# Key/value, query and recurrent output products taken from high and low parts of their operands

## What is computed

```
h = x
layer 0: xn = rms_norm(h);  q, f, i, g = split(xn @ hgrn_w_in)        # 1024 x 4096
         o  = chunkwise gated recurrence(silu(q), key(f), i, decay(f))  # 8 heads of 128
         h += (rms_norm(o) * silu(g)) @ hgrn_w_out                      # 1024 x 1024
         h += swiglu(rms_norm(h))                                       # dense, 2816 wide
shared:  kv = rms_norm(h) @ kv_w                                        # 1024 x 1536
         compressed, selected and window keys and values from kv
layer 1: proj = rms_norm(h) @ nsa_w_in                                  # 1024 x (1024 + 48 gates)
         h += attention(three branches, gated) @ nsa_w_out
         h += top-2-of-8 experts (each 3584 wide) of rms_norm(h)
```

## Time and profile before

| | us |
|---|---|
| median of 3 runs (1558.01 to 1558.24) | 1558.22 |
| the profiled execution's own time | 1556.34 |
| its span, first to last instruction | 1554.8 |
| TensorE (PE) busy | 1521.5 (98%) |
| VectorE (DVE) busy | 1127.9 (73%) |
| ScalarE (ACT) busy | 938.3 (60%) |
| GpSimd (POOL) busy | 56.2 (4%) |
| mean granted clock of TensorE | 0.996 |

### The profile page before, as it was taken

One profiled execution on the slowest core, in us unless ns is written; L12 is line 12 of the kernel. 1 busy time (PEld: TensorE's weight loads), 2 busy tenths in 40 slices (PEclk: granted clock), 3 DMA queues, 4 the chain that ended last, 5 costly groups with the idle time before them and its releaser, 6 DMA issues.

```text
span 1554.8 us, 19505 instructions
## 1 busy us (share of the span) xinstructions
PE 1521.5 (98%) x6905; PEld 1182.5 (76%) x6905; DVE 1127.9 (73%) x988; ACT 938.3 (60%) x946; POOL 56.2 (4%) x83
## 2 busy tenths in 40 slices
PE   7999999999999998999999999999999999999998
PEld 6866578887455647888888888888888888888886
DVE  1077455554326837888888889888888888888997
ACT  4323344443213435778778778778778778778775
POOL 2000100000101001000000000000000000000100
PEclk9999999999999999999999999999999999999999
DMA  9833155448575017999999999999999999999994
GB/s 363 282 109 100 53 179 202 170 148 218 200 296 189 1 35 262 378 369 367 396 388 357 395 384 356 394 382 365 393 388 357 393 386 355 394 394 348 398 393 181
DMA packets 213023, 455.53 MB, mean 293 GB/s; under 512 B 9857, under 2 KB 36522, under 8 KB 212970
## 3 DMA queue, kind: packets, MB, share of 16 engines
q1 hardware_dynamic: 206624, 441.48, 78.2%
q0 software_dynamic: 3536, 12.96, 2.1%
q10 hardware_dynamic: 2810, 0.40, 0.1%
HBM read 434.89 MB, written 19.92 MB: 293 GB/s over the span
## 4 chain that ended last, share of the span: by engine, by line
PE 95%; DVE 3%; POOL 1%; issue 0%; DMA 0%; ACT 0%; DVEq 0%; POOLq 0%
PE bank L2079 59%; PE bank L1714 8%; PE bank L1731 4%; PE bank L1608 4%; PE bank L1641 4%; PE bank L1777 3%; PE bank L1946 2%; PE bank L1630 2%; PE bank L1664 2%; PE bank L2099 2%; PE bank L1840 1%; PE bank L1814 1%; DVE small L1308 1%; PE bank L1915 1%; PE bank L1888 1%; POOL small L539 0%
## 5 line engine op out<-in xcount | busy, mean ns | idle before, releaser
L1467 DVE TENSOR_TENSOR w_lo<-ring,w_hi 128x2048 fp32r<-128x2048 f32 x333 | 756.3, 2290 | 104.8 <-ACT w_hi L900 104.1
L900 ACT ACTIVATE w_hi<-ring 128x2048 fp32r<-128x2048 f32 x333 | 638.0, 1921 | 169.6 <-PE bank L2079 166.5
L2079 PE MATMUL bank<-w_hi,x_hi 128*128 128x512 f32 x896 | 244.3, 394 | 0.6 <-DVE x_lo L1475 0.6
L2079 PE MATMUL bank<-w_hi,x_lo 128*128 128x512 f32 x896 | 240.0, 390 | 0.0
L2079 PE MATMUL bank<-w_lo,x_hi 128*128 128x512 f32 x896 | 239.7, 389 | 0.0
L2079 PEld LDWEIGHTS bank<-w_hi,x_lo 128*128 128x128 f32 x896 | 168.2, 188 | 35.9
L2079 PEld LDWEIGHTS bank<-w_lo,x_hi 128*128 128x128 f32 x896 | 168.2, 188 | 35.2
L2079 PEld LDWEIGHTS bank<-w_hi,x_hi 128*128 128x128 f32 x896 | 164.5, 188 | 32.3 <-issue 0.8
L1073 DVE TENSOR_TENSOR ring_lo<-ring,f_whi 128x1024 fp32r<-128x1024 f32 x66 | 80.6, 1225 | 87.0 <-ACT f_whi L734 87.0
L2079 PE MATMUL bank<-w_hi,t_hi 128*128 128x512 f32 x448 | 122.6, 395 | 0.0
L2079 PE MATMUL bank<-w_hi,t_lo 128*128 128x512 f32 x448 | 121.1, 392 | 0.0
(11 more groups left out here) (276 smaller groups left out, 1486.3 us busy)
## 6 DMA issues: line engine op xcount, KB each, us to landing
ring<-in_moe_w_gu SPq DMA_DIRECT2D x224, 1024.0 KB, 7.6
ring<-in_moe_w_down SPq DMA_DIRECT2D x112, 1024.0 KB, 8.1
ring<-in_ffn_w_gu SPq DMA_DIRECT2D x22, 1024.0 KB, 6.5
ring<-in_hgrn_w_in SPq DMA_DIRECT2D x16, 1024.0 KB, 15.3
ring<-in_ffn_w_down SPq DMA_DIRECT2D x10, 1024.0 KB, 6.9
x_rows<-arena SPq DMA_DIRECT2D x2, 4096.0 KB, 21.6
ring<-in_kv_w SPq DMA_DIRECT2D x6, 1024.0 KB, 6.2
ring<-in_hgrn_w_out SPq DMA_DIRECT2D x4, 1024.0 KB, 11.1
```

Source lines behind the costliest of these rows:

```text
L900: act.activation(w_hi[s % PARTS][:, :], raw[:, s % RAWS, :], ACT.Copy).then_inc(hi_ready, 1)
L1467: dve.tensor_tensor(w_lo[s % PARTS][:, :], raw[:, s % RAWS, :], w_hi[s % PARTS][:, :].bitcast(F32), ALU.subtract).then_inc(lo_ready, 1)
L2079: last = mm(out_, x_[k], w[:, k, 512 * b:512 * b + 512], start=start and k == 0 and n == 0, stop=stop and k == HALF // width - 1 and n == 2)
```

## The change

The three plain products are taken from parts as well: each 8 matmuls of a product become 24, in two halves of 12 (four `k`, three kinds). Weights are parted in quarters of an item (128x1024).

- Recurrent output: ACT makes eight high quarters behind its copies of rounds 4 to 7 of the recurrence, into slots 4 and 5; DVE subtracts them in rounds 5 to 8, one behind each group's `ops_ready`. The low part of the rows is made by DVE, one step of 128x512 for each quarter of the rows, behind `on_ready`. Items 11 and 12 of the dense weights, which go into these slots, wait for the third and the fourth output product.
- Keys and values: ACT makes the rows' high part (`rows_high`) once all of the dense layer's output is there, DVE the low part, and the high weight quarters lie in the arena (the first six) and in slots whose item has been used (free at `kv_ps` 2 and 4, ...). The last four transposes of h stand inside the first product. `cin` waits for `kv_ps` 4 as well.
- Queries: high and low parts of the rows are copies of 128x1024 each, twice, behind `kv_ps` 6; the eight weight quarters follow `kv_ps` 4 to 6.
- POOL clears its block only behind `kv_ps` 4; SP issues the zeroing ahead of the output weights; these now wait for `q_ps` 4, and so do the first expert weights (before: `q_ps` 3).
- The small transfers are issued later, in round 2 of ACT's key/value loop; positions stay on `misc_in` (32), the other three go to `wr_in`, awaited just ahead of the gates.

```diff
         def left(i):
+            if i in (4, 5):
+                return res_ps, i - 1
...
             if i < I_CMP:
-                return kv_ps, 2 * (i - I_KV) + 2
+                return q_ps, 4
...
+            pool.wait_ge(kv_ps, 4)
             pool.memset(b_zero, 0.0).then_inc(zero_made, 1)
...
+                if n >= 4:
+                    for s in (2 * n - 8, 2 * n - 7):
+                        if s < 8:
+                            i = I_HOUT + s // 4
+                            act.wait_ge(slot_full[i % SLOTS], full(i))
+                            act.wait_ge(proj_ready, 10 + 2 * (s // 4))
+                            act.activation(o_quarter(s)[2], o_quarter(s)[0], ACT.Copy).then_inc(o_hi, 1)
...
+            def weight_high(*ss):
+                for s in ss:
+                    i = n_item(s)
+                    act.wait_ge(slot_full[i % SLOTS], full(i))
+                    act.wait_ge(*n_free(s))
+                    act.activation(n_high(s), n_quarter(s)[0], ACT.Copy).then_inc(q_hi, 1)
...
+            weight_high(0, 1, 2, 3)
+            rows_high(0)
+            rows_high(1)
+            rows_high(2)
+            rows_high(3)
             squared(2, 0, 6)
             squared(2, 1, 8)
+            weight_high(4, 5)
+            act.wait_ge(xT_dve, 8)
             shared_turned(1, G_MIX1, xT)
+            act.wait_ge(xT_dve, 10)
             shared_turned(3, G_MIX1, xT)
             for j in range(6):
+                if j == 1:
+                    weight_high(6, 7)
+                if j == 2:
...
+                    weight_high(8, 9)
...
+                if j == 3:
+                    weight_high(10, 11)
+                if j == 4:
+                    weight_high(12, 13)
                 act.wait_ge(kv_ps, j + 1)
...
+            query_rows_high(0)
+            weight_high(14, 15)
+            query_rows_high(1)
+            weight_high(16, 17, 18, 19)
...
+                    if 5 <= n:
+                        s = 2 * (n - 5) + grp
+                        dve.wait_ge(o_hi, s + 1)
+                        dve.tensor_tensor(o_quarter(s)[1], o_quarter(s)[0], o_quarter(s)[2].bitcast(F32),
+                                          ALU.subtract).then_inc(o_lo, 1)
...
+            weight_low(0, 1, 2)
             residual(4, 0)
             residual(4, 1)
-            shared_turned(0, G_KV, b_xk)
             residual(4, 2)
             residual(4, 3)
-            shared_turned(2, G_KV, b_xk)
+            weight_low(3)
+            rows_low(0)
+            rows_low(1)
+            rows_low(2)
+            rows_low(3)
             shared_turned(0, G_MIX1, xT)
+            weight_low(4, 5)
             shared_turned(2, G_MIX1, xT)
+            weight_low(6, 7)
...
+            dve.wait_ge(kv_ps, 2)
+            weight_low(8, 9)
             key_normed(0)
+            weight_low(10, 11)
...
+            weight_low(12, 13)
             key_turned(0)
             key_normed(2)
             key_turned(1)
+            query_rows_low(0)
+            weight_low(14, 15)
             key_normed(3)
+            query_rows_low(1)
+            weight_low(16, 17)
             key_turned(2)
             key_turned(3)
+            weight_low(18, 19)
...
             def shared(j):
                 it, tb = divmod(j, 2)
+                for a in range(2):
+                    s = 4 * it + 2 * a
+                    if j == 0 and a == 1:
+                        turned(2)
+                        turned(3)
+                    pe.wait_ge(q_hi, N_QUART + s + 2)
+                    pe.wait_ge(f_x_ok, 4 + 2 * tb + a + 1)
+                    wh, wl = halves_of_item(s)
+                    for kind, (x_, w) in enumerate(((n_xhi, wh), (n_xhi, wl), (n_xlo, wh))):
+                        if kind == 1:
+                            pe.wait_ge(q_lo, N_QUART + s + 2)
+                        if kind == 2:
+                            pe.wait_ge(xT_dve, 6 + 2 * tb + a + 1)
+                        for k in range(4 * a, 4 * a + 4):
+                            last = mm(bank[:, KV_BANK[j], :], x_[:, k, P * tb:P * tb + P], w[k % 4], ...)
```

More of the change, by code:

```diff
@@ L771, in shared_turned, with rows_high @@
                 last.then_inc(xT_act, 1)
-            shared_turned(1, G_KV, b_xk)
-            shared_turned(3, G_KV, b_xk)
+            def weight_high(*ss):
[4 more added lines that the diff above has]
+                    act.activation(n_high(s), n_quarter(s)[0], ACT.Copy).then_inc(q_hi, 1)
+            def rows_high(j):
+                tb, k0 = j // 2, 4 * (j % 2)
+                act.wait_ge(res_ps, 8)
+                act.wait_ge(xT_ps, 9 + j)
+                for k in range(k0, k0 + 4):
+                    last = act.activation(n_xhi[:, k, P * tb:P * tb + P], bank[:, j, P * (k - k0):P * (k - k0) + P],
+                                          ACT.Copy, scale=gain[:, G_KV + k:G_KV + k + 1])
+                last.then_inc(f_x_ok, 1)
@@ L775, in _, with query_rows_high @@
+            def query_rows_high(half):
+                act.wait_ge(kv_ps, 6)
+                act.wait_ge(xT_dve, 12)
+                act.wait_ge(xT_act, 4)
+                act.activation(q_xhi[:, 4 * half:4 * half + 4, :], xT[:, 4 * half:4 * half + 4, :],
+                               ACT.Copy).then_inc(f_x_ok, 1)
+            weight_high(0, 1, 2, 3)
[3 more added lines that the diff above has]
+            rows_high(3)
             squared(2, 0, 6)
             squared(2, 1, 8)
+            weight_high(4, 5)
@@ L1066, in _ @@
                                   ALU.mult).then_inc(on_ready, 1)
+                for i in {1: (0,), 2: (1,), 3: (2, 3)}.get(j, ()):
+                    dve.wait_ge(oT_act, i + 1)
+                    at = slice(4 * (i % 2), 4 * (i % 2) + 4), slice(P * (i // 2), P * (i // 2) + P)
+                    dve.scalar_tensor_tensor(o_xlo[:, at[0], at[1]], bank[:, 4 + i, :].rearrange("p (k t) -> p k t", k=4),
+                                             gain[:, G_HG:G_HG + 1], o_xhi[:, at[0], at[1]].bitcast(F32),
+                                             ALU.mult, ALU.subtract).then_inc(oT_lo, 1)
             quarters = [0]
@@ L1211, in _ @@
             dve.wait_ge(pos_ready, 1)
+            dve.wait_ge(kv_ps, 4)
             for g in range(NG):
@@ L1766, in _, with turned, halves_of_item @@
                 down_quarter(f)
-            for j in range(4):
+            def turned(j):
                 pe.wait_ge(h_ready, 5 + j)
                 turn_block(h, j // 2, 4 * (j % 2), j, xT_ps)
+            turned(0)
+            turned(1)
+            def halves_of_item(s):
+                high, low = [], []
+                for d in (s, s + 1):
+                    for v, to in ((n_high(d), high), (n_quarter(d)[1], low)):
+                        to += [v[:, 512 * k:512 * k + 512] for k in range(2)]
+                return high, low
             def shared(j):
                 it, tb = divmod(j, 2)
-                if tb == 0:
-                    arrived(I_KV + it)
-                for k in range(KD):
-                    last = mm(bank[:, KV_BANK[j], :], b_xk[:, k, P * tb:P * tb + P], cols(I_KV + it)[:, k, :],
-                              start=k == 0, stop=k == KD - 1)
+                for a in range(2):
+                    s = 4 * it + 2 * a
[6 more added lines that the diff above has]
+                    for kind, (x_, w) in enumerate(((n_xhi, wh), (n_xhi, wl), (n_xlo, wh))):
+                        if kind == 1:
+                            pe.wait_ge(q_lo, N_QUART + s + 2)
+                        if kind == 2:
+                            pe.wait_ge(xT_dve, 6 + 2 * tb + a + 1)
+                        for k in range(4 * a, 4 * a + 4):
+                            last = mm(bank[:, KV_BANK[j], :], x_[:, k, P * tb:P * tb + P], w[k % 4],
+                                      start=k == 0 and kind == 0, stop=k == KD - 1 and kind == 2)
                 last.then_inc(kv_ps, 1)
@@ L1978, in _ @@
             turn(0)
-            query(3, range(4, 8))
+            query(3, (1,))
             copied(0)
```

141 lines of the change are left out of this document (101 added, 40 removed).

## The result

| | before | after |
|---|---|---|
| median (lowest to highest of 4 runs each), us | 1558.12 (1557.66 to 1558.24) | 1546.68 (1545.51 to 1547.52) |
| ratio of the two, 95% interval | | 0.9932 (0.9919 to 0.9945) |
| the profiled execution's own time, us | 1556.34 | 1545.51 |
| its span, us | 1554.8 | 1543.9 |
| mean granted clock of TensorE in it | 0.996 | 0.994 |

The forecast was 1545.7 us; the change is faster by 11.4 us (1558.12 - 1546.68), where 12.5 were forecast. That it lies so near is partly luck, and it hides two errors: the keys, values and queries gave what they should, the recurrence gave less (1.4 us instead of 2.3), and a stretch that was to stay as it is, the attention, grew by 1.4 us.

The account below looks back on a forecast made before the run. TensorE, busy 98% of the span, was taken as the bound. Savings of 2.3 (recurrence), 6.9 (keys, values) and 3.3 (queries) sum to 12.5: 1558.22 - 12.5 = 1545.7 us, range 1543.5 to 1548 (8 in 10: 1541 to 1551.5).

Parts of the forecast that it names:

- Price of a product: Each changed product: 24 matmuls at 0.231 us take 5.55 us instead of 6.87, saving 1.32.
- Recurrent output: Recurrence to dense start: four products save 5.3 us, last round loses 2.6, before the last half 0.4; net 2.3 saved.
- the walk: Recurrence's last round, step by step: ACT's exponentials 0.6 us late, last pairs at 157.6, first output product 2.6 late.
- The rival of the falling clock: Clock falls where TensorE idles in the recurrence's last round: up to 2 us lost, 1547.5 us; chance 0.20.
- its 0.4: Recurrent output, before the last half: DVE makes two low row quarters before the addition the next transposes need; 0.4 us lost.
- Keys and values: Six products save 1.32 us each, 0.8 gained at the start, 0.7 and 1.1 lost to waits; net 6.9 saved.
- the third item's low quarters: Keys and values: DVE makes them behind the first key's norm, which waits for POOL; TensorE loses 1.1 us.
- that of the second item: Keys and values: TensorE waits for the second item's late quarters because ACT runs late; 0.7 us lost.
- Queries: First two products save 1.32 us each, the third's second half 0.66, the fourth nothing; sum 3.3 saved.
- From here everything moves together: After the queries, the attention onward merely starts earlier; the DVE chain there is untouched, no change in length.
- Hidden parts: Zeroing, output and expert weights, and small transfers stay hidden at zero cost; compression's blocks ready by less than 1 us.
- four signs of being wrong: Matmuls above 0.24 us, clock below 1 around 157, weight waits in the SwiGLU's second chunk, or a longer attention.

Follow-up runs that it names:

- warm_tail: Changed kernel plus ten zero-weight matmuls between the two groups of pairs of the recurrence's last round; median 1544.90 us, 0.9928 of before.
- again: The changed kernel itself, unedited, measured once more on another chip; median 1547.90 us, 0.9939 of before.
- pool_early: Changed kernel with POOL clearing its block behind the second product of keys and values instead of the fourth; median 1547.92 us, 0.9937 of before.
- warm_attn: Changed kernel plus ten zero-weight matmuls at the attention's start, where TensorE idles behind the last query product; median 1542.82 us, 0.9916 of before.
- q3_one: Changed kernel with the fourth query product from high parts alone, 8 matmuls instead of 24; median 1546.28 us, 0.9931 of before.
- all_three: Changed kernel with the edits of tail_moved, pool_early and warm_attn together; median 1540.75 us, 0.9890 of before; repeated on a third chip, 1540.97 us, 0.9904.
- tail_moved: Changed kernel with the last two high quarters and DVE's two subtractions moved out of the recurrence's last round; median 1544.41 us, 0.9918 of before.
- all_filled: all_three with gate matmuls split around half the first query product, warm_tail's filling, and eight zero matmuls at the attention's second idle place; 1540.80 us, 0.9898 of before.

## Why the prediction was right, and where not

**Price of a product: right.** 5.51 to 5.55 us for 24 matmuls. The trace has 0.230 us a matmul. An estimate by the 215.7 ns of the Trainium skill (TensorE: Matmul & The Clock Gate, Part 1, "Wait — 56ns, not 53.3ns?") would have had 5.18 (24 x 0.2157), 6% too low for this type.

**Recurrent output: the mis-sized term.** Forecast -2.3 us, measured -1.4. Each step of the walk came out (0.41 for 0.6, pairs at 157.54 for 157.6), and the working priced the matmuls behind them at the full clock. The rival of the falling clock had 0.20 and 0.9 to 2 us; here the two groups took 0.92 (2.08 - 1.16) and 0.66 (1.57 - 0.91) longer, partly beside other work, and warm_tail wins back 0.66 of the stage. With the clock up, that is, the part gives 2.07 (47.56 - 45.49). The other 0.2 of the miss is not the clock's: one half of a product runs while ACT and DVE work toward the next transposes (from 188.41 to 192.42 before, from 187.77 to 191.78 after, 4.01 us both times), so that making it cheaper gains nothing, and seven halves give 4.6 us (7 x 0.66) where 5.3 - 0.4 = 4.9 was in the sum. The forecast's reason for its 0.4, DVE's low quarters of the rows ahead of the addition, does not show. All five profiled executions whose last round is as changed and unfilled have this fall (after, again, pool_early, warm_attn, q3_one), and of the other seven changed versions only one (all_three). The forecast had the idle stretch (152.5 to 159.5) and the row that shows what follows one, and still left it out of the sum. It should have been in the sum, and the last two quarters out of the last round: tail_moved shows that the choice of place, with the fall that it brings, not the product from parts, cost 3.2 us of 4.6 that the four products could give (47.56 - 42.92).

**Keys and values: right.** Forecast -6.9, measured -7.05. The first product starts 1.82 us behind the SwiGLU's end (386.11 - 384.29), forecast 1.7. The wait for the third item's low quarters is 1.03 us against 1.1; that of the second item, forecast at 0.7, does not show among TensorE's waits. It was overstated by ACT's walk, which is a little faster than the 1.1 us a quarter I took (1.99 for two in the chain).

**Queries: right.** Forecast -3.3, measured -3.45; q3_one confirms that the fourth product is worth nothing.

**"From here everything moves together": failed.** The attention is 76.46 us before and 77.84 after. Of its instructions only those of the last query product changed, with which TensorE is done sooner: it idles 2.48 us behind it, where in the kernel before its idle time was 1.14. Four marks in it show what the clock takes: the first scores, the matmul behind this idle time, the one behind the second (2.00 us in both kernels), and the end. Without a fall (warm_tail) the parts are 16.94, 9.41 and 48.31 us. Before has 16.92, 9.42 and 50.12, with its one fall behind the second idle time; after has 16.93, 10.99 and 49.92, with a fall behind each. So the new idle time brought a fall of 1.58 us, which the kernel before did not have in its profiled execution. Read over all thirteen profiled executions, the length goes by the number of falls: none 74.64, 74.65 and 74.66; one 76.06, 76.22 and 76.46; two 77.83 to 77.86, four times; three 80.52. A fall costs 1.4 to 2.7 us. (all_filled and q3_one are apart, one for its filling, the other for one fall of 10 us.) So this stage was never 76.46 long by its work: 1.8 of it was clock.

**Hidden parts: right.** No wait of TensorE for a transfer shows in the trace from 195 to 480 us, and DVE's blocks to be compressed come 0.9 us ahead of the compression (419.01 + 4.14 against 424.06), where "less than 1 us" of slack was forecast.

**Experts and front:** -0.45 and +0.11, which no step explains; two executions of one kernel differ by 0.7 in the experts and by up to 1.4 ahead of the first mark (148.79 and 150.19, the two of all_three, on two chips).

Sum: forecast 12.5, less 0.9 in the recurrence, less 1.4 in the attention, plus 0.15 + 0.15 + 0.45 in the rest, less 0.1 in front, is 10.85, against 10.9 of the spans. The medians say 11.4, and the forecast in time was 1.0 us low. Of that nearness 0.45 is the experts' and 0.5 the difference of medians and spans, neither of which the forecast had a step for, and on the second chip the gain is 9.0. Of the forecast's four signs of being wrong two came true, the clock below 1 around 157 and the longer attention: the price, the walk and the keys, values and queries were right, and that the clock stays up behind a longer idle stretch, which the sum took without a term for it, was not.

The Trainium skill (TensorE: Matmul & The Clock Gate, Part 1, "What's actually happening") says that the throttled state is the default and that how much of it a kernel meets is "run-variable". The second half agrees with these runs: the same idle stretch of 2.48 us with and without a fall. pool_early's fall at 442 us stands behind a row in which TensorE is busy for 2.00 of 2.00 us, and no run here shows what brought it.

What stays open: whether the small matmuls of the gates are the cause of the fall behind them, and what decides, from one execution to the next, whether an idle stretch of 2 us is followed by one. The kernel before was profiled once, so that its single fall in the attention is one case; its mean clocks on the other chips (mostly 0.995 to 0.997, against 0.991 to 0.994 of the changed kernel) say that it has fewer or shorter ones as a rule.

## What to carry to other kernels

When a product gets cheaper, walk on to the next place where its engine waits: the time won becomes idle time there, and the clock may charge for it (1.6 us here, and 0.7 in the recurrence), so price matmuls behind a stretch of idle TensorE at both levels. Put the steps that part weights where no round ends by them, also if that is later than the slot allows: moving two quarters out of the recurrence's last round was worth more in that stage (3.2 us) than the four cheaper products had left in it (1.4). Where versions differ by less than a fall costs, compare the medians of several runs beside each run's granted clock, and not two profiled executions.

## What the runs showed of the hardware

The time of an execution follows its mean granted clock: pool_early's five runs have 1543.18 us at 0.995 and 1547.91 to 1548.47 at 0.992; an estimate from the mean clock, 0.003 of 1545 us, is 4.6, and 4.7 to 5.3 were measured. A fall came behind idle stretches of 2.0 to 2.5 us (157, 480 and 491 us) in most but not all executions; more rarely behind shorter ones (0.83 and 1.27 us in all_three, 1.25 and 0.46 in tail_moved); and also behind 32 matmuls of 48 columns with TensorE fully busy (442 us). Matmuls with zero weights kept the clock up: with them at the attention's first idle place no fall came there in five executions, without them one came in six of seven. One fall cost 0.7 us (after against warm_tail) and 1.2 us (all_three and its repetition) in the recurrence, and 1.4 to 1.8 in the attention; the parting of 128x1024 weights took ACT 1.0 us and DVE 1.14 us (two in 1.99, one in 1.14).
